# The recurrent mixer of a two-block transformer: the convolved half of its projection first, the gates between its tiles

## The reference, cut to what matters

```
def rglru_mixer(u, w_in, b_in, conv_w, conv_b, w_gx, b_gx, w_ga, b_ga, lam, w_out, b_out):
    proj = u @ w_in + b_in                                   # 1024 -> 2 x 1280
    ybr = gelu(proj[..., :LRU_WIDTH])                        # the y half
    xbr = causal_dwconv(proj[..., LRU_WIDTH:], conv_w, conv_b)   # the convolved half
    xh = xbr.reshape(bsz, s, LRU_HEADS, LRU_BLOCK)           # 10 heads of 128
    gx = sigmoid(einsum('bshi,hij->bshj', xh, w_gx) + b_gx)
    ga = sigmoid(einsum('bshi,hij->bshj', xh, w_ga) + b_ga)
    log_a = LRU_C * ga * log_sigmoid(lam)
    a_t = exp(log_a)
    b_t = sqrt(-expm1(2.0 * log_a)) * gx * xbr
    h = scan over the tokens of h = a_t * h + b_t
    return (h * ybr) @ w_out + b_out
```

## Time and profile before

| | us |
|---|---|
| median of 3 executions | 2552.93 (2550.88 to 2553.77) |
| the profiled execution | 2551.12 |
| its span | 2549.3 |
| PE busy | 2193.8 (86% of the span) |
| DVE busy | 916.1 (36%) |
| ACT busy | 363.1 (14%) |

### The profile page before, as it was taken

The page is one execution under the profiler, slowest core; times in us unless marked ns, Lnnn a source line. Parts: engine busy times, 40 slices in busy tenths (PEclk is TensorE's granted clock), DMA queues, the critical chain, the costliest instruction groups (busy, mean ns, idle before and its releaser), DMA issues.

```text
span 2549.3 us, 28377 instructions
## 1 busy us (share of the span) xinstructions
PE 2193.8 (86%) x11468; PEld 1540.3 (60%) x11468; DVE 916.1 (36%) x2034; ACT 363.1 (14%) x724; POOL 1.2 (0%) x16
## 2 busy tenths in 40 slices
PE   6999999997666666666666799999999998999999
PEld 4778888862222222222222288778888877788887
DVE  6796896131001100000100175626131336523233
ACT  2231111120000000000000022501010124101011
POOL 0000000000000000000000000000000000000000
PEclk9999999998888888878888899999999999999999
DMA  7526564469999999999999963044344431454420
GB/s 277 185 70 228 204 225 132 165 274 428 428 428 428 429 429 429 428 428 428 429 428 428 415 234 132 34 165 162 135 165 142 154 120 50 165 184 147 165 99 17
DMA packets 147476, 638.13 MB, mean 250 GB/s; under 512 B 10277, under 2 KB 52782, under 8 KB 119486
## 3 DMA queue, kind: packets, MB, share of 16 engines
q1 hardware_dynamic: 146446, 634.79, 63.4%
q10 hardware_dynamic: 944, 2.13, 0.2%
HBM read 635.86 MB, written 1.05 MB: 250 GB/s over the span
## 4 chain that ended last, share of the span: by engine, by line
PE 66%; DMA 27%; DVE 4%; ACT 2%; issue 1%; ACTq 0%; DVEq 0%; SPq 0%
DMA arena<-in_w_down_dram 19%; PE PS L1731 16%; PE PS L1131 13%; PE PS L1744 8%; PE PS L1044 7%; DMA arena<-in_w_up_dram 5%; DMA arena<-in_w_gate_dram 3%; PE PS L1498 3%; PE PS L1561 2%; PE PS L1517 2%; PE PS L1361 2%; DVE arena L1849 2%; PE PS L1695 2%; PE PS L1532 1%; PE PS L1489 1%; PE PS L1804 1%
## 5 line engine op out<-in xcount | busy, mean ns | idle before, releaser
L1498 PE MATMUL PS<-arena,hT 128*32 128x512 f32 x2048 | 304.2, 736 | 163.2 <-DMA arena<-in_w_up_dram 136.0
L1731 PE MATMUL PS<-arena 128*128 128x256 f32 x1920 | 416.7, 379 | 0.0
L1731 PEld LDWEIGHTS PS<-arena 128*128 128x128 f32 x1920 | 364.6, 190 | 49.8
L1498 PEld LDWEIGHTS PS<-arena,hT 128*32 128x32 f32 x2048 | 65.7, 124 | 383.5 <-DMA arena<-in_w_up_dram 212.6
L1131 PE MATMUL PS<-hT,arena 128*128 128x256 f32 (+1 forms) x1136 | 253.6, 383 | 1.5 <-ACT hT L717 1.5
L1517 PE MATMUL PS<-arena,hT 128*32 128x512 f32 x1008 | 171.5, 817 | 94.8 <-DMA arena<-in_w_down_dram 87.7
L1849 DVE SCALAR_TENSOR_TENSOR arena<-arena 128x512 f32<-128x512 f32 (+2 forms) x514 | 246.4, 547 | 0.8
L1131 PEld LDWEIGHTS PS<-hT,arena 128*128 128x128 f32 (+1 forms) x1136 | 213.3, 190 | 39.3 <-issue 9.7
L1846 DVE TENSOR_SCALAR arena<-arena,cols 128x256 f32<-128x256 f32 x162 | 66.3, 409 | 413.4 <-ACT arena L961 358.2
L1852 DVE TENSOR_TENSOR hT<-hT,PS 128x512 f32<-128x512 f32 x16 | 16.4, 1027 | 507.1 <-PE PS L1498 507.1
L1744 PE MATMUL PS<-arena 128*128 128x256 f32 x896 | 195.9, 379 | 0.0
(11 more groups left out here) (296 smaller groups left out, 1793.6 us busy)
## 6 DMA issues: line engine op xcount, KB each, us to landing
arena<-in_w_gate_dram SPq DMA_DIRECT2D x64, 2048.0 KB, 41.1
arena<-in_w_up_dram SPq DMA_DIRECT2D x64, 2048.0 KB, 40.9
arena<-in_w_down_dram SPq DMA_DIRECT2D x63, 2048.0 KB, 37.6
arena<-in_ffn_w_up_dram SPq DMA_DIRECT2D x32, 2048.0 KB, 8.5
arena<-in_w_in_dram SPq DMA_DIRECT2D x36, 1024.0 KB, 7.9
arena<-in_ffn_w_down_dram SPq DMA_DIRECT2D x16, 2048.0 KB, 7.9
arena<-in_w_ada_dram SPq DMA_DIRECT2D x12, 2048.0 KB, 11.7
arena<-in_ssd_w_in_dram SPq DMA_DIRECT2D x10, 2048.0 KB, 9.5
```

Of the source, the lines that this page charges most:

```text
L1498: mm = pe.matmul(PS[32 * f:32 * f + 32, 1 + half, :], xe[:, 32 * (2 * pi + k):32 * (2 * pi + k) + 32], w[:, k, 512 * f:512 * f + 512], sta ...
L1731: mm = pe.matmul(PS[:, n, T * half:T * half + T], slot(TAIL_SLOT[j], 8, 512)[:, k, P * n:P * n + P], hs[:, k, :], start=(k == 0), stop=(k ...
```

## The change

The halves of the projection change places: tiles 0 to 9 are now the convolved half and 10 to 19 the y half (panel 2 straddles them and is loaded by two DMAs). PE computes the gates of two heads behind each of tiles 9, 10, 11, 12 and 13, into banks 4 to 7. ACT copies seven of the ten y tiles without a function, takes the sigmoids pair by pair between, then all twenty Exp and Tanh with three of those copies among them, all ten square roots, and then one Gelu over seven tiles (1792 columns); the last three y tiles go through Gelu one by one. DVE runs the ten scans on end, with the multiplication by y five heads behind.

```diff
+TWO_LOADS = (("lru_g", 0), ("lru_in", 2))
+FIRST_GATES, N_Y_GELU = 9, 7
...
             for j in range(5):
-                load("lru_in", j, at("lru_in", j, 8, 512), lru_w_in[:, :, 512 * j:512 * j + 512])
+                c = LRU_W + 512 * j if j < 2 else 512 * j - LRU_W
+                dst = at("lru_in", j, 8, 512)
+                if j == 2:
+                    load("lru_in", 2, dst[:, :, 0:256], lru_w_in[:, :, 2 * LRU_W - 256:2 * LRU_W])
+                    sp.dma_start(dst[:, :, 256:512], lru_w_in[:, :, 0:256]
+                                 ).then_inc(slot_in[ST.slots["lru_in"][2]], 16)
+                else:
+                    load("lru_in", j, dst, lru_w_in[:, :, c:c + 512])
...
+            for t in range(NL):
+                c = COL["lru_b_in_2"] + NL + t
                 if t < 4:
                     act.wait_ge(s["raw_ev"], 4 * PRE.index("mix_pre1") + t + 1)
+                    src = pads[:, t, 3:3 + T]
                 else:
                     act.wait_ge(*tile_done(s, used, "ly_ps", ["lru_in"], t - 3))
+                    act.wait_ge(s["lcv_done"], t - 3)
                     src = PS[:, t % 4, 0:T]
+                act.activation(pads[:, t % 4, 3:3 + T], src, ACT.Identity, bias=cols[:, c:c + 1]
+                               ).then_inc(s["ly_ready"], 1)
+            def y_tile(t):
+                m, c = NL + t, COL["lru_b_in_2"] + t
+                act.wait_ge(*tile_done(s, used, "ly_ps", ["lru_in"], m - 3))
+                act.activation(yb[:, t, :], PS[:, m % 4, 0:T], ACT.Identity if t < N_Y_GELU else ACT.Gelu_apprx_tanh,
                                bias=cols[:, c:c + 1]).then_inc(s["ly_ready"], 1)
+            def gate_act(h):
+                act.wait_ge(s["lg_gate_ps"], h + 1)
                 for half, (dst, b) in enumerate(((gx, "lru_b_gx_2"), (ga, "lru_b_ga_2"))):
+                    act.activation(dst[:, h, :], PS[:, 4 + h % 4, T * half:T * half + T], ACT.Sigmoid,
                                    bias=cols[:, COL[b] + h:COL[b] + h + 1]).then_inc(s["lsig"], 1)
+            for h in range(0, NL, 2):
+                gate_act(h)
+                gate_act(h + 1)
+                if h < NL - 2:
+                    y_tile(h // 2)
...
+            for h in range(NL):
+                act.activation(la[:, h, :], ga[:, h, :], ACT.Exp, scale=lam_c[:, h:h + 1]).then_inc(s["la_act"], 1)
+                act.activation(lt[:, h, :], ga[:, h, :], ACT.Tanh, scale=lam_d[:, h:h + 1]).then_inc(s["la_act"], 1)
+                if h in (4, 8, 9):
+                    y_tile((4, 8, 9).index(h) + 4)
+            for h in range(NL):
+                act.wait_ge(s["lb_chain"], 2 * h + 2)
+                act.activation(lt[:, h, :], lt[:, h, :], ACT.Sqrt).then_inc(s["lb_sqrt"], 1)
+            act.wait_ge(s["ly_ready"], NL + N_Y_GELU)
+            act.activation(yb[:, 0:N_Y_GELU, :], yb[:, 0:N_Y_GELU, :], ACT.Gelu_apprx_tanh).then_inc(s["ly_ready"], 1)
+            for t in range(N_Y_GELU, NL):
+                y_tile(t)
...
+            for m in range(4, 2 * NL):
...
+                if m >= 8:
+                    pe.wait_ge(s["ly_ready"], m - 3)
+                mm = tile(PS[:, n, 0:T], [(w[:, k, P * n:P * n + P], hs[:, k, :]) for k in range(KD)],
+                          norm=None if m > 4 else "mix_pre1")
...
+                if 0 <= m - FIRST_GATES < NL // 2:
+                    for h in (2 * (m - FIRST_GATES), 2 * (m - FIRST_GATES) + 1):
+                        lru_gate(h).then_inc(s["lg_gate_ps"], 1)
+            pe.wait_ge(s["lsig"], 2 * NL)
             open_rows()
...
+            def times_y(h):
+                dve.wait_ge(s["ly_ready"], NL + N_Y_GELU + 1 if h < N_Y_GELU else NL + h + 2)
+                tt(xb[:, h, :], ga[:, h, :], yb[:, h, :], ALU.mult).then_inc(s["lh_ready"], 1)
+            for h in range(NL):
+                dve.wait_ge(s["lb_sqrt"], h + 1)
+                link("mix_tmp", tt(gx[:, h, :], gx[:, h, :], lt[:, h, :], ALU.mult))
+                link("mix_tmp", dve.tensor_tensor_scan(ga[:, h, :], la[:, h, :], gx[:, h, :], 0.0, ALU.mult, ALU.add))
+                if h >= NL // 2:
+                    times_y(h - NL // 2)
+            for h in range(NL // 2, NL):
+                times_y(h)
```

More of the change, by code:

```diff
@@ L164, in __init__ @@
                 else:
-                    put(name, TAIL_SLOT[nxt], p, 2 if name == "lru_g" else 1)
+                    put(name, TAIL_SLOT[nxt], p, 2 if (name, j) in TWO_LOADS else 1)
                 p, nxt = p + 1, (nxt + 1) % RING_TAIL
@@ L1773, in _, with lru_gate @@
             raw_tiles("mix_pre1", slot(ST.slots["lru_in"][0], 8, 512), [("mix_pre1", sq, 5)]).then_inc(used, ST.incs["lru_in"][0])
[L1776 to L1781, removed]
             g = ST.slots["lru_g"][0]
-            pe.wait_ge(slot_in[g], ST.need["lru_g"][0])
-            pe.wait_ge(s["ly_ready"], 20)
-            for h in range(NL):
+            def lru_gate(h):
                 pe.wait_ge(s["lcv_done"], h + 1)
@@ L1788, in _ @@
                     pe.wait_ge(s["lsig"], 2 * (h - 3))
[L1789 to L1793, removed]
-                else:
-                    mm.then_inc(used, ST.incs["lru_g"][0])
-            pe.wait_ge(s["raw_ev"], 4 * PRE.index("mix_pre1") + 4)
+                pe.matmul(PS[:, 4 + h % 4, 0:T], slot(g, NL, P)[:, h, :], xb[:, h, :], start=True, stop=True)
+                return pe.matmul(PS[:, 4 + h % 4, T:512], slot(g, NL, P, NL * P)[:, h, :], xb[:, h, :],
+                                 start=True, stop=True)
+            for m in range(4, 2 * NL):
+                j, n = m // 4, m % 4
+                w = slot(ST.slots["lru_in"][j], 8, 512)
+                if n == 0:
+                    arrived("lru_in", j)
+                if m >= 8:
+                    pe.wait_ge(s["ly_ready"], m - 3)
+                mm = tile(PS[:, n, 0:T], [(w[:, k, P * n:P * n + P], hs[:, k, :]) for k in range(KD)],
+                          norm=None if m > 4 else "mix_pre1")
+                if n < 3:
+                    mm.then_inc(s["ly_ps"], 1)
+                elif j == 4:
+                    mm.then_inc(used, ST.incs["lru_in"][j] + ST.incs["lru_g"][0])
+                else:
+                    mm.then_inc(used, ST.incs["lru_in"][j])
+                if m == FIRST_GATES:
+                    pe.wait_ge(slot_in[g], ST.need["lru_g"][0])
+                    pe.wait_ge(s["raw_ev"], 4 * PRE.index("mix_pre1") + 4)
+                if 0 <= m - FIRST_GATES < NL // 2:
+                    for h in (2 * (m - FIRST_GATES), 2 * (m - FIRST_GATES) + 1):
+                        lru_gate(h).then_inc(s["lg_gate_ps"], 1)
+            pe.wait_ge(s["lsig"], 2 * NL)
             open_rows()
@@ L1801, in _ @@
                 for k in range(4):
-                    pe.wait_ge(s["lh_ready"], 2 * (4 * j + k) + 2)
+                    pe.wait_ge(s["lh_ready"], 4 * j + k + 1)
                     for n in range(KD):
@@ L2476, in _ @@
             post_dve("ffn_post0", gain_of("norm_ffn_post_2"), "mix_pre1", gain_of("norm_mix_pre_2", 8))
[L2477 removed]
+            raw_scale("mix_pre1", "lru_in", lambda n: pads[:, n, 3:3 + T], rstd[:, :])
             for t in range(NL):
[L2481 to L2482 removed]
+                dve.wait_ge(s["ly_ready"], t + 1)
+                conv4(t, pads[:, t % 4, :], xb[:, t, :], "lru_conv_w_2", NL, "lru_conv_b_2", t,
                       "dve_chain").then_inc(s["lcv_done"], 1)
@@ L2487, in _ @@
                 link("mix_tmp", tt(gx[:, h, :], gx[:, h, :], xb[:, h, :], ALU.mult))
[L2488 to L2500, removed]
+            for h in range(NL):
+                dve.wait_ge(s["la_act"], 2 * h + 2)
+                tt(ga[:, h, :], la[:, h, :], la[:, h, :], ALU.mult).then_inc(s["lb_chain"], 1)
+                dve.wait_ge(s["lb_chain"], 2 * h + 1)
+                stt(lt[:, h, :], ga[:, h, :], 1.0, lt[:, h, :], ALU.add, ALU.mult).then_inc(s["lb_chain"], 1)
+            def times_y(h):
+                dve.wait_ge(s["ly_ready"], NL + N_Y_GELU + 1 if h < N_Y_GELU else NL + h + 2)
+                tt(xb[:, h, :], ga[:, h, :], yb[:, h, :], ALU.mult).then_inc(s["lh_ready"], 1)
+            for h in range(NL):
+                dve.wait_ge(s["lb_sqrt"], h + 1)
[5 more added lines that the diff above has]
+                times_y(h)
             post_dve("mix_post1", gain_of("norm_mix_post_2", 8), "ffn_pre1", gain_of("norm_ffn_pre_2", 8),
```

9 lines of the change are left out of this document (2 added, 7 removed).

## The result

| | kernel before | changed kernel |
|---|---|---|
| median | 2553.35 us (4 executions) | 2537.62 us (4 executions, 2537.17 to 2542.29) |
| profiled execution, span | 2551.12, 2549.3 | 2537.88, 2536.1 |
| later comparison on one chip | 2553.12 (11) | 2539.33 (5, 2537.18 to 2544.02) |

The ratio is 0.9947, 95% interval 0.9932 to 0.9961, and 0.9948 (0.9936 to 0.9961) in the later comparison. The forecast was 2541.0, in a range from 2537.5 to 2546.5, so the first median lies only 0.12 us above the range's lower end.

The account below looks back on a forecast made before the run. The prediction saw PE setting nothing for 19.32 us, behind ACT's and DVE's chain between two projections. 9.71 + 1.94 = 11.65 us off the profiled 2551.12 gave 2539.5, 2541.3 as a median, lowered to 2541.0; range 2537.5 to 2546.5.

Parts of the forecast that it names:

- PE's own end: Mixer projection on PE: gates add 8.64 us, opening rows follow, PE free at 2145.40, output projection starts 9.71 us earlier.
- No stall between the tiles: Projection tiles with gates between them: PE never waits for ACT or DVE; 0 us, bounds 0 and 1.
- ACT's chain: ACT beside the projection: sigmoids, Exp/Tanh, square roots and one Gelu of 1.69 us, ending at 2143.0.
- The slack: Before the output projection: DVE's product allows a start at 2144.8, PE is free at 2145.4; 0.6 us to spare.
- The clock: Output projection's first matmuls: PE's idle nearly gone, so they run at 2.4 GHz, saving 1.94 us more.
- The restart at the norm: Norm after the change: PE's restart price after idle taken as unchanged, could move by -3.2 to +1 us.
- The added load: ACT leaving the mixer: an extra 1.28 us table load before the root, hidden in 1.64 us; 0, bounds 0 and 1.3.
- DMA: Weight panel loads: same bytes, one panel in two halves, all issued well before use; taken as 0 us.

Follow-up runs that it names:

- lag_0: Changed kernel with DVE multiplying by y right behind each head's scan instead of five heads behind; 2537.83 us, ratio 0.9950 to the kernel before.
- first_8: Changed kernel with the pairs of gates behind tiles 8 to 12 instead of 9 to 13; 2540.05 us, ratio 0.9951 to the kernel before.
- first_10: Changed kernel with the pairs of gates behind tiles 10 to 14 instead of 9 to 13; 2543.11 us, ratio 0.9964 to the kernel before.
- first_12: Changed kernel with the pairs of gates behind tiles 12 to 16 instead of 9 to 13; 2551.89 us, ratio 1.0001 to the kernel before.
- before_warm: Kernel before with 38 matmuls of zeros between the opening rows and the output projection; 2550.24 us, ratio 0.9994.
- after_2: Changed kernel run again unaltered, on the same chip as its version with filled norm gaps; 2539.33 us.
- gates_last: Changed kernel with all ten heads' gates on PE behind tile 19 again and all sigmoids there; 2561.75 us, ratio 1.0039 to the kernel before.
- after_warm_2: Second run of the changed kernel with 18 matmuls of zeros in each of three idle norm gaps; 2534.70 us, ratio 0.9929 to the kernel before.
- gelu_each: Changed kernel with every y tile taken through Gelu where it is copied, no single 1792-column Gelu; 2549.01 us, ratio 0.9989 to the kernel before.
- after_warm: Changed kernel with 18 matmuls of zeros in each of three idle norm gaps, first run; 2534.07 us, ratio 0.9927 to the kernel before.

## Why the prediction was right

1. *PE's own end.* Forecast: the gates cost PE 8.64 us and the opening rows 0.97 in its path, start 9.71 us earlier. Measured 9.74. The term was right, and with it that PE sets the start: lag_0 shows that an earlier operand changes nothing, and first_8 how close DVE is.
2. *No stall between the tiles.* Right: PE is busy for 65.00 of the 65 us from 2080 to 2145.
3. *ACT's chain.* Forecast on the old scale: end of the sigmoids 2124.6, of the Exp/Tanh 2135.4, of the square roots 2140.0, of the Gelu 2143.0. With 0.46 added, the changed kernel's rows give 2124.56, 2135.10, 2139.57 and 2142.59. The Gelu of 1792 columns, which no row had, took 1.70 us for 1.69. The error is 0.4 us over 20, on the safe side: 0.3 of it in the twenty Exp/Tanh with three copies (9.17 us, not 9.4), 0.1 in the ten square roots (3.17, not 3.3).
4. *The slack.* 0.6 us forecast on DVE, 0.86 found. first_10 and first_12, whose starts were worked out from it, came within 0.2 us.
5. *The clock.* 1.94 us forecast for the output projection, 1.75 measured; before_warm shows that it is the clock. The 0.2 us lie in the length at full clock: 27.82 in the trace, not the 27.63 of 128 x 0.2159. By the same step the norms' 48 matmuls take 10.60 at full clock, not 10.36, so the two restarts of rows 8 had cost 1.6 and 3.0 us, not 1.9 and 3.2. The restart at the norm, left unchanged with bounds from -3.2 to +1, moved by -1.28 in the profiled execution.
6. *The added load.* Hidden, with 0.34 us over (0.36 by the sum). The drain that the Trainium skill ("ScalarE: Activation LUTs", section "What ACT_TABLE_LOAD costs") adds to each load is not in this kernel either: a sigmoid group that ends at 2122.40 + 1.70 = 2124.10 is followed by its load at 2124.18, and the Exp behind that starts at 2125.47, 1.37 us in all. The measurement decides.
7. *DMA.* No row of the changed kernel's chain in this stretch is DMA.

What was off is a size: 11.65 us were forecast between executions, and the medians lie 13.3 to 15.7 apart. In the profiled pair the surplus is 1.6 us: 1.28 for the restart behind the mixer and 0.46 from work ahead of it, less 0.16 in the terms above. Neither is the change's own. I took the restart at the norms from one execution, and gave 0.3 us for its variation. The 48 raw matmuls took 12.0 to 12.3 us in some profiled executions and 12.9 to 13.7 in others (at the three norms 12.03, 12.26 and 12.29 in the changed kernel's first profile, 13.66, 13.09 and 12.93 in after_2), so each restart moves by 0.6 to 1.6 us with no change in the code.

The restarts are not the whole of the variation. Between the two profiles of the changed kernel they make 3.1 of 4.5 us. But in seven profiled executions with the same code up to there (the changed kernel, after_2, gates_last, first_8, first_10, first_12, lag_0) the first of the three restarts begins at 1716.76 to 1724.65 us, 7.9 us apart before any of them is paid; and after_warm_2, which does not pay them, spreads as widely as the changed kernel. What varies there was not traced. My reading of 2553.35 against 2537.62 as 15.7 us is likely too much by 2; the later comparison, with 13.8, is nearer to the traces' 11.5 for the start and the output projection. How the remaining 2 divide between restarts and the rest of the program isn't settled. So the mechanism was forecast well, and that the first median fell inside the range, by 0.12 us, was partly luck.

## What to carry to other kernels

Look for a chain of small steps on a slow engine between two dense stretches of the matrix engine, and start it from the middle of the first stretch. That costs the matrix engine the small products it used to do for free, here 8.6 us and 1 us of opening rows, and removes 19.3 us in which it set nothing. The chain's end could here be forecast to half a microsecond by adding up rows, as long as every waiting instruction was placed in its engine's order; where one was not, in first_8, the forecast failed. The same chain, with fewer table loads but longer batches, was slower than the old one when left in the open, so move first and batch second. And where the matrix engine must be idle for a few microseconds in front of dense work, try filling the gap with matmuls into an unused bank: three gaps gave 3.6 and 4.6 us in two comparisons.

## What the runs showed of the hardware

- In one execution each, the clock's price did not follow the length of the idle: 2.61 us of idle behind the opening rows cost the output projection 1.7 us, 5.86 cost 2.2, 7.07 cost 1.8, 8.89 cost 1.7 and 17.79 cost 2.3, all against 27.87 us in first_8, where 0.25 us of idle cost nothing. The restarts at the norms moved by up to 1.6 us with no change in the code, so the order among these five is not shown. In first_10 the granted clock was still 0.92 in the microsecond in which PE restarted (2154.12), and 0.50 in the next. The Trainium skill, "TensorE: Matmul & The Clock Gate", section "HAM oscillation — how this bites in real kernels", describes waits for operands between groups of matmuls that bring the clock down, so that the next group starts slow. Here an idle of 2.61 us was enough, and the fall came when PE was already busy again.
- Matmuls of zeros in bf16 held the clock at 1.00 as well as real ones: 38 of them in the gap of 8.9 us (before_warm), 18 in each gap of 4.4 to 4.5 us (after_warm).
- Table loads cost nothing where ACT was waiting for PE anyway: with two in each period of 5.18 us ACT still had 0.53 us of idle (gelu_each). Behind tile 13, where six more loads than in the changed kernel stood on the chain, the chain came 8.0 us later (7.1 and the slack of 0.86).
